# Last branch products of the third block: two output tiles a weight piece, eight sums open at once

## The reference

```python
y_a = o_a.reshape(Bn, L, GLA_V) @ lp['w_pa']
...
o_b = o_b.reshape(Bn, L, SSM_INNER) * jax.nn.silu(z)
o_b = rms_norm_3(o_b.reshape(Bn, L, SSM_GROUPS, SSM_INNER // SSM_GROUPS), ...)
y_b = o_b @ lp['w_pb']
merged = jax.nn.sigmoid(gate_a) * y_a + jax.nn.sigmoid(gate_b) * y_b
return merged @ lp['w_out'], (st_af, st_ab, st_bf, st_bb)
```

## Time and profile before

| | |
|---|---|
| median of three runs | 3487.12 us |
| profiled execution | 3491.64 us, of which 3489.6 us span |
| mean granted TensorE clock in it | 0.963 |
| PE busy | 3258.9 us, 93% of the span |
| DVE, POOL, ACT busy | 2117.2, 1371.3, 1249.0 us |

### The profile page before, as it was taken

How to read it: one execution, slowest core, us unless ns; L and a number is a source line. 1 busy time by engine, 2 the same in 40 slices (tenths; PEclk the granted TensorE clock), 3 DMA queues, 4 the chain that set the end, 5 groups by cost and what they waited for, 6 DMA issues and landing times. The chain is left out here.

```text
span 3489.6 us, 44690 instructions
## 1 busy us (share of the span) xinstructions
PE 3258.9 (93%) x17806; PEld 2622.1 (75%) x17806; DVE 2117.2 (61%) x2504; ACT 1249.0 (36%) x1899; POOL 1371.3 (39%) x625
## 2 busy tenths in 40 slices
PE   8999998999998998999999999888989868899998
PEld 6778777888866677977888877767877646678886
DVE  6586865889865476354756554868982777631112
ACT  4233343323344332333423342334441654332222
POOL 3434343444432233435344433326641322334443
PEclk9999999999999999999999999999999979999999
DMA  3223353465333245444444222533333755422322
GB/s 120 91 85 125 123 172 131 168 233 179 132 113 97 79 132 156 129 164 156 148 145 151 96 98 88 176 97 125 105 113 115 231 156 151 154 85 83 106 92 76
DMA packets 237662, 451.26 MB, mean 129 GB/s; under 512 B 59936, under 2 KB 120032, under 8 KB 230416
## 3 DMA queue, kind: packets, MB, share of 16 engines
q1 hardware_dynamic: 230384, 437.93, 38.8%
q10 hardware_dynamic: 7072, 10.49, 0.8%
HBM read 396.88 MB, written 51.46 MB: 128 GB/s over the span
## 5 line engine op out<-in xcount | busy, mean ns | idle before, releaser
L288 POOL TENSOR_TENSOR stream_feed_lo<-stream_feed_raw,stream_feed_hi 128x1024 fp32r<-128x1024 f32 (+4 forms) x555 | 1255.8, 2265 | 2013.4 <-ACT stream_feed_hi L281 1959.5
L281 ACT ACTIVATE stream_feed_hi<-stream_feed_raw 128x1024 fp32r<-128x1024 f32 (+4 forms) x555 | 533.3, 963 | 707.5 <-PE ffn_low L188 174.9
L186 PE MATMUL shared_ps<-third_h_hi,stream_feed_hi 128*128 128x512 f32 (+1 forms) x776 | 322.1, 415 | 39.2 <-ACT third_in_rows_bend L794 17.1
L187 PE MATMUL shared_ps<-third_h_lo,stream_feed_hi 128*128 128x512 f32 (+1 forms) x776 | 311.3, 401 | 0.0
L188 PE MATMUL shared_ps<-third_h_hi,stream_feed_lo 128*128 128x512 f32 (+1 forms) x776 | 311.3, 401 | 0.0
L186 PE MATMUL mixer_acc<-first_h_hi,stream_feed_hi 128*128 128x512 f32 x544 | 222.2, 408 | 7.2 <-DVE first_h_lo L1406 5.4
L480 DVE SCALAR_TENSOR_TENSOR ffn_ada_sum<-ffn_ada_w,cond,ffn_ada_sum 128x512 f32<-128x512 f32 x196 | 219.0, 1134 | 4.1
L186 PEld LDWEIGHTS shared_ps<-third_h_hi,stream_feed_hi 128*128 128x128 f32 (+1 forms) x776 | 151.1, 195 | 85.6 <-issue 44.3
L188 PE MATMUL mixer_acc<-first_h_hi,stream_feed_lo 128*128 128x512 f32 x544 | 214.2, 394 | 0.0
L187 PE MATMUL mixer_acc<-first_h_lo,stream_feed_hi 128*128 128x512 f32 x544 | 214.1, 394 | 0.0
L186 PE MATMUL ffn_low<-ffn_mid_hi,stream_feed_hi 128*128 128x512 f32 x528 | 207.6, 393 | 4.7 <-DVE x_res L702 4.6
(11 more groups left out here) (767 smaller groups left out, 7243.0 us busy)
## 6 DMA issues: line engine op xcount, KB each, us to landing
stream_feed_raw<-in_stream SPq DMA_DIRECT2D x406, 512.0 KB, 3.4
ffn_ada_w<-in_w_ada SPq DMA_DIRECT2D x48, 1024.0 KB, 5.4
stream_feed_raw<-in_stream SPq DMA_DIRECT2D x50, 384.0 KB, 3.1
stream_feed_raw<-in_stream SPq DMA_DIRECT2D x52, 256.0 KB, 3.0
stream_feed_raw<-in_stream SPq DMA_DIRECT2D x36, 320.0 KB, 3.0
scratch_gates<-mixer_gate ACTq DMA_DIRECT2D x32, 256.0 KB, 2.1
mix_gin<-scratch_gates SPq DMA_DIRECT2D x32, 256.0 KB, 3.2
x_res<-scratch_cum SPq DMA_DIRECT2D x16, 512.0 KB, 7.6
```

What stands on the lines that cost most here:

```text
L186: nc.tensor.matmul(out, w_hi, x_hi, start=start, stop=False)
L187: nc.tensor.matmul(out, w_hi, x_lo, start=False, stop=False)
L281: self.nc.scalar.activation(self.hi[:, p % self.cut, :n], self.raw[:, p % self.deep, :n], ACT.Copy).then_inc(self.cut_hi, 1)
L288: eng.tensor_tensor(self.lo[:, p % self.cut, :n], self.raw[:, p % self.deep, :n], self.hi[:, p % self.cut, :n].bitcast(F32), ALU.subtract) ...
```

## The change

- The second half of `w_pb` is stored in other pieces: a piece holds 4 input tiles (one group) for two output tiles. The first four pieces (numbers 16 to 19 of the stage) hold group 2 for output tiles 0 and 1, 2 and 3, 4 and 5, 6 and 7; the next four (20 to 23) hold group 3 likewise. The amount of weights and of products is the same.
- `tensor_last` opens eight sums in eight banks (0, 1, 2, 3, 4, 6, 7, 5): the group 2 halves of all eight output tiles, with `sums(3)` ahead of the fourth (m = 3), and then the group 3 halves of all eight. Each bank has its own wait for what used it before (`freeing`).
- A piece is `used` after its second output tile. Evictions of even tiles wait for a new semaphore, `closed`, and those of odd tiles for the piece.
- ACT splits piece 20 between the squares and the root.
- SP's program issues the gates of q 16 and 17, then all loads that the stage still needs, and then the other gates.

```diff
-        return self.acc[:, q % 4 if q >= 2 * DT else q % 2]
+        return self.acc[:, (0, 1, 2, 3, 4, 6, 7, 5)[q - 2 * DT] if q >= 2 * DT else q % 2]
...
+    def tensor_last(self, pe, freeing, sums, before_sums):
+
+        def halves(part, m):
+            if m % 2 == 0:
+                self.w[0] = self.feed.take(pe, *self.pieces[2 * DT + DT // 2 * part + m // 2])
+            w_hi, w_lo = self.w[0]
             for k in range(DT // 2):
...
+                at, of = DT // 2 * part + k, DT // 2 * (m % 2) + k
+                if m == 0:
+                    self.wait_input(pe, 2 * DT, at)
+                last = product(self.nc, self.bank(2 * DT + m), (w_hi[:, of], w_lo[:, of]),
+                               (self.h[0][:, at], self.h[1][:, at]), at == 0, at == DT - 1)
+            if m % 2:
+                self.feed.spent(last)
+            elif part:
+                last.then_inc(self.closed, 1)
+
+        for m in range(DT):
+            if m == before_sums:
                 sums()
...
+            freeing(m)
+            halves(0, m)
+        for m in range(DT):
+            halves(1, m)
...
-            self.feed.done(dve, *self.pieces[q])
+            m = q - 2 * DT
+            if m < 0:
+                self.feed.done(dve, *self.pieces[q])
+            elif m % 2:
+                self.feed.done(dve, *self.pieces[2 * DT + DT // 2 + m // 2])
+            else:
+                dve.wait_ge(self.closed, m // 2 + 1)
...
+                dense.sync_gates(sp, 2 * DT)
+                dense.sync(sp, 3 * DT)
                 for q in range(2 * DT, 3 * DT):
                     dense.sync_gates(sp, q)
-                    dense.sync(sp, q)
                 sp.wait_ge(x_back, 16)
...
-                dense.tensor_last(pe, 1, lambda: (pe.wait_ge(y_made, 16), sums(3)))
+
+                def freeing(m):
+                    if m < 2:
+                        pe.wait_ge(dense.freed, 2 * DT - 1 + m)
+                    if m == 2:
+                        pe.wait_ge(read, 30)
+                    if m == 3:
+                        pe.wait_ge(read, 31)
+                    if m == 5:
+                        pe.wait_ge(y_made, 16)
+                    if m == 7:
+                        pe.wait_ge(meaned, 4)
+
+                dense.tensor_last(pe, freeing, lambda: (pe.wait_ge(y_made, 16), sums(3)), 3)
...
+                dense.scalar(act, 2 * DT)
                 square(3)
-                dense.scalar(act, 2 * DT)
+                dense.scalar(act, 2 * DT + 1)
                 root(3)
...
+    wide = i["w_pb_3"][0]
+    for m in columns:
+        add("pb3", [wide[k * P:(k + 1) * P, m:m + P] for k in range(DT)])
+    for n in (DT, DT + DT // 2):
+        for two in zip(columns[::2], columns[1::2]):
+            add("pb3", [wide[k * P:(k + 1) * P, m:m + P] for m in two for k in range(n, n + DT // 2)])
```

More of the change, by code:

```diff
@@ L3777, in __init__ @@
         self.part = core.sumsq
-        self.cut, self.lesser, self.freed, self.gated = (s.sem(n) for n in ("cut", "lesser", "freed", "gated"))
+        self.cut, self.lesser, self.freed, self.gated, self.closed = (
+            s.sem(n) for n in ("cut", "lesser", "freed", "gated", "closed"))
         self.gate_in = [s.sem(f"gate_in{n}") for n in range(2)]
@@ L3815, in wait_input @@
         pe.wait_ge(self.lesser, q + k + 1)
[L3817 to L3824, removed]
-            for k in range(DT // 2):
[L3826 to L3829, removed]
-                sums()
[L3831 to L3844, removed]
+    def tensor_last(self, pe, freeing, sums, before_sums):
[3 more added lines that the diff above has]
+            w_hi, w_lo = self.w[0]
+            for k in range(DT // 2):
+                at, of = DT // 2 * part + k, DT // 2 * (m % 2) + k
[9 more added lines that the diff above has]
+            if m == before_sums:
+                sums()
+            freeing(m)
+            halves(0, m)
+        for m in range(DT):
+            halves(1, m)
     def sync_gates(self, sp, evicted):
@@ L4134, in _ @@
                         fill(g, 1, c)
-                pe.wait_ge(read, 30)
-                dense.tensor_last(pe, 1, lambda: (pe.wait_ge(y_made, 16), sums(3)))
+                def freeing(m):
[10 more added lines that the diff above has]
+                dense.tensor_last(pe, freeing, lambda: (pe.wait_ge(y_made, 16), sums(3)), 3)
             @block.scalar
@@ L4547, in stream @@
     by_row("pa3", i["w_pa_3"][0], columns)
-    for n in (0, DT):
-        for m in columns:
-            add("pb3", [i["w_pb_3"][0][k * P:(k + 1) * P, m:m + P] for k in range(n, n + DT)])
+    wide = i["w_pb_3"][0]
[4 more added lines that the diff above has]
+            add("pb3", [wide[k * P:(k + 1) * P, m:m + P] for m in two for k in range(n, n + DT // 2)])
     by_row("out3", i["w_out_3"][0], columns)
```

## The result

Twelve runs of the changed kernel gave a median of 3495.22 us, twelve of the kernel before 3488.14: 7.1 us more, a ratio of 1.0021 (95% interval 1.0012 to 1.003). A second comparison gave 1.0020 (1.001 to 1.0029). That lies inside the 0.3% that was called no change, on the slow side of it, and inside the range of 3484 to 3499 us; the forecast was 3493.0, 5.9 us more.

A forecast was written before the change was run, and what follows sets the result against it. PE was busy 93% of the span, but SP's in-order queue was taken to decide: PE done 4.4 us sooner, late gates ending the stage 5.9 us later. Added to the median of 3487.12: 3493.0 us, range 3484 to 3499.

The forecast's parts named there:

- PE's end: Last product of the stage on PE starts 4.4 us sooner: 2.7 for moved products, 1.7 for the low-parts gap.
- rival (b): Late gates hold, but PE's clock stays at 2.4 GHz through the sums: plus 3.9 us, 3491.0; chance 20%.
- The queue: SP's late gates wait behind eight weight loads, first issued at 3046.87; the stage ends 5.9 us later.
- two bounded prices: Landing times of late gate loads: 3.4 us for the first two, 2.7 for the others, bounds 2.0 and 3.8.
- Rival (a): SP's queue does not block, gates are in time and PE sets the end: minus 4.4 us, 3482.7; chance 5%.
- rival (c): Same gate chain with longer landings, averaging 4.5 us or more: slower by more than 10.5 us; chance 10%.
- The next stage: Merge stage behind the barrier: takes on the whole delay, first matmul 1.8 us after the last addition.
- its clock loss: Start of the next stage at 1.2 GHz loses some 2.9 us, taken as unchanged.
- Edits at nothing: ACT's and POOL's splits, bank waits and the `closed` counter in the stage: between 0 and 0.2 us, taken as 0.

The follow-up runs named there:

- second comparison: The changed kernel, unaltered, run once more against the kernel before: median 3495.55 us, ratio 1.0020.
- the run with the gates further forward: Changed kernel with sums ahead of the sixth tile and late gate loads placed early among the weight loads, against the kernel before: 3479.83 us, ratio 0.9975.

## Why the prediction was right

**PE's end.** Forecast 4.4 us sooner, measured 5.0. All three parts are there: the 12 products ahead of the sums, no gap for low parts, and the last sum still behind the fourth square (the first product follows it by 1.14 us in both). The two waits for squares stayed, as 2.32 and 0.70 us instead of the two of some 1.4 named under rival (b). The 0.6 is the clock. In the profile after the granted clock, columns as in the earlier trace rows, is 0.50 from 3004 to 3010 and 0.90 at 3010 to 3012:

```profile
3002.00:3004.00 2.00, 0.00 (x0) 0.00 (x0) 1.26 (x2) 0.63 (x1) 0.00 (x0) 0.89 0.96 325
3008.00:3010.00 2.00, 2.00 (x6) 1.19 (x5) 1.07 (x2) 0.98 (x1) 2.00 (x1) 0.50 0.70 285
3010.00:3012.00 2.00, 2.00 (x9) 1.61 (x8) 2.00 (x1) 0.00 (x0) 0.12 (x1) 0.90 0.45 135
```

It returned some 2.5 us after the first product behind the sums instead of 3.3. Rival (b), a clock that stays up, did not happen here, but it is what the sums ahead of the sixth tile do.

**The queue.** The first gate was issued 36.91 us after the fourth square, forecast 3046.87 - 3009.29 = 37.58; most of the 0.67 is the clock again. The two bounded prices were close:

```profile
sq<-scratch_gates SPq DMA_DIRECT2D x2, 256.0 KB, 3.7
```

```profile
sq<-scratch_gates SPq DMA_DIRECT2D x4, 256.0 KB, 2.6
```

The first row is the pair behind the weight load (3.4 taken between 2.0 and 3.8), the second the other four (2.7 taken). The end came at 50.39 against 50.65 forecast, so the tail's 5.6 against 5.9. That is closer than its parts, by luck: the start came 0.67 early, the first landing cost 0.26 more than taken, and the pair of evictions behind it 1.55 us instead of 1.44. The two runs that move only the order of the queue show that this is the cause: 11.7 us off when the gates go forward, 10.6 of them the queue's, and 9.5 to 11.1 on when the old kernel's go back. Rival (a) is refuted by the wait of 17.12 us in the changed kernel itself; in rival (c) landings would have had to average 4.5 us, and in the changed kernel's two profiles none of these took over 3.7.

**The next stage.** It started 1.8 us behind the last addition as before, and from its first to its last matmul took 46.27 us against 46.08. Leaving its clock loss as it was came out right for this pair, which is luck in part: in six of the other eight profiles it took about 45.0, both kernels' second executions among them, so a us or so comes and goes there.

**Edits at nothing.** ACT's split of piece 20 ran from 3006.64 to 3007.68 and the root came at 3013.01, 6.28 us after the fourth square both before and after. No wait for a bank or a piece appears on PE.

What was weak is the size of what a comparison of times can see: 5.6 us of the tail became 7.1 in the median, and a prediction for this kernel cannot be tested finer than that without the profile's own anchors.

## What to carry to other kernels

A DMA queue's program is in order, and a load that waits for a slot keeps back everything written behind it; so place each transfer by when its own wait ends, and check for each small load which waits stand ahead of it. When PE has a wait, fill it with products that need nothing new until the awaited thing is there, and count up to where it is: here the sums ahead of the sixth tile, which left no wait for a square, gave a stage 4.1 us shorter than those ahead of the fourth. Measure a few us in 3500 from an event in the same trace, not from the span.

## What the runs showed of the hardware that was not expected

Gate transfers of 256 KB took 2.7 us (median, kernel before) and 2.6 (changed kernel) one or two at a time; six issued about 0.47 us apart behind a weight load took 3.5 to 5.5 us, with a median of 5.0.

A DVE addition of two operands in SBUF, 0.69 us where POOL is idle, took 2.69 us when it began during a split by POOL, and ended 0.55 us after that split (3032.62 against 3032.07); the eviction ahead of it, with one operand in PSUM, kept its 0.69. From the run with the gates further forward:

```profile
3029.20 0.69 DVE L3876 SCALAR_TENSOR_TENSOR sumsq<-sq,shared_ps 128x512 f32<-128x512 f32 x1 [1.75 <-DMA sq<-scratch_gates]
3029.93 2.69 DVE L3881 TENSOR_TENSOR third_merged<-third_merged,sumsq 128x512 f32<-128x512 f32 x1
3032.76 0.69 DVE L3876 SCALAR_TENSOR_TENSOR sumsq<-sq,shared_ps 128x512 f32<-128x512 f32 x1
```

```profile
3026.87 5.20 POOL L288 TENSOR_TENSOR stream_feed_lo<-stream_feed_raw,stream_feed_hi 128x1024 fp32r<-128x1024 f32 x2
3032.58 2.40 POOL L288 TENSOR_TENSOR stream_feed_lo<-stream_feed_raw,stream_feed_hi 128x1024 fp32r<-128x1024 f32 x1 [0.51 <-ACT stream_feed_hi L281]
```

The Trainium skill (GPSIMD Engine Reference, the first table) says that the two engines share SBUF interfaces and contend where a DVE instruction has two SBUF inputs; the trace agrees, with 2.0 us for one addition. It cost nothing here: DVE had caught up by the seventh tile, where it waited 0.92 us for PE.
